# Output matrices that begin with the rows already at hand, and a head norm taken by group

## The reference, cut to what matters

```
# even mixer (layer 0)
o = o_fwd + o_bwd                                  # delta rule, 8 heads of 128
o = o * rsqrt(mean(o*o, -1) + eps) * out_gain
y_dn = o * silu(gate)                              # 1024 columns
y_sc = b_gate * centred_dwconv(c_gate * u_in)      # 1024 columns, no delta result in it
return concatenate([y_dn, y_sc]) @ w_out           # [256, 2048] @ [2048, 2048]

# odd mixer (layer 1)
y_c = sum(wts * outs)                              # attention, 512 columns
y = ys[0] + ys[1]                                  # RWKV both ways, 8 heads of 64
yn = (y - mean) * rsqrt(var + eps) * ln_w + ln_b   # mean, var over a head
y_d = (yn + bonus) * gate                          # 512 columns
return concatenate([y_c, y_d]) @ w_out             # [256, 1024] @ [1024, 2048]
```

## Time and profile before

| | us |
|---|---|
| three runs | 3073.96, 3075.31, 3089.07 |
| median | 3075.31 |
| profiled execution, its own time | 3086.94 |
| span of the profiled execution | 3084.9 |
| PE busy | 2899.5 (94%) |
| DVE busy | 1569.9 (51%) |
| ACT busy | 1270.4 (41%) |
| POOL busy | 186.1 (6%) |
| mean granted PE clock | 0.955 |

### The profile page before, as it was taken

How to read it: one execution, slowest core, us unless ns; L and a number is a source line. 1 busy time by engine, 2 the same in 40 slices (tenths; PEclk the granted TensorE clock), 3 DMA queues, 4 the chain that set the end, 5 groups by cost and what they waited for, 6 DMA issues and landing times.

```text
span 3084.9 us, 45243 instructions
## 1 busy us (share of the span) xinstructions
PE 2899.5 (94%) x18708; PEld 2662.6 (86%) x18708; DVE 1569.9 (51%) x1923; ACT 1270.4 (41%) x1564; POOL 186.1 (6%) x169
## 2 busy tenths in 40 slices
PE   7999989899999999999899986888799999999999
PEld 7999988788898989899798984888688989898897
DVE  4555455555554454444545556443655444544444
ACT  4543322364543534444444443112455434444343
POOL 0000055100000000000000001432000000000000
PEclk9999989899999999999999997877899999999999
DMA  6455300254455455555445550001344545545444
GB/s 250 165 191 183 132 1 1 109 178 150 151 191 192 179 195 187 191 184 186 150 174 187 193 177 17 1 1 55 109 164 141 187 178 179 193 175 191 178 179 149
DMA packets 67915, 462.26 MB, mean 150 GB/s; under 512 B 7007, under 2 KB 10079, under 8 KB 12940
## 3 DMA queue, kind: packets, MB, share of 16 engines
q1 hardware_dynamic: 63680, 449.95, 40.7%
q10 hardware_dynamic: 3500, 5.21, 0.5%
q0 software_dynamic: 544, 4.19, 0.4%
HBM read 457.21 MB, written 5.27 MB: 150 GB/s over the span
## 4 chain that ended last, share of the span: by engine, by line
PE 91%; DVE 5%; ACT 2%; issue 1%; POOL 0%; DMA 0%; ACTq 0%; DVEq 0%; POOLq 0%
PE bank L401 13%; PE bank L402 13%; PE bank L403 13%; PE bank L376 12%; PE bank L378 12%; PE bank L377 12%; PE bank L1020 3%; PE bank L1004 3%; PE bank L1988 1%; PE bank L1211 1%; PE bank L502 1%; ACT split_hi L320 1%; DVE hT_lo L515 0%; DVE split_lo L327 0%; PE bank L1709 0%
## 5 line engine op out<-in xcount | busy, mean ns | idle before, releaser
L327 DVE TENSOR_TENSOR split_lo<-raw,split_hi 128x1024 fp32r<-128x1024 f32 x840 | 1026.6, 1225 | 1113.2 <-ACT split_hi L320 1112.3
L320 ACT ACTIVATE split_hi<-raw 128x1024 fp32r<-128x1024 f32 x840 | 888.2, 1059 | 1312.9 <-PE bank L403 696.8
L401 PE MATMUL bank<-hT_hi,split_hi 128*128 128x256 f32 x3376 | 963.2, 285 | 23.0 <-issue 11.4
L402 PE MATMUL bank<-hT_lo,split_hi 128*128 128x256 f32 x3376 | 961.3, 285 | 0.0
L403 PE MATMUL bank<-hT_hi,split_lo 128*128 128x256 f32 x3376 | 961.1, 285 | 0.0
L401 PEld LDWEIGHTS bank<-hT_hi,split_hi 128*128 128x128 f32 x3376 | 654.4, 194 | 26.8 <-issue 17.9
L402 PEld LDWEIGHTS bank<-hT_lo,split_hi 128*128 128x128 f32 x3376 | 654.5, 194 | 0.2
L403 PEld LDWEIGHTS bank<-hT_hi,split_lo 128*128 128x128 f32 x3376 | 654.3, 194 | 0.0
L376 PE MATMUL bank<-split_hi,u_hi 128*128 128x512 f32 x1152 | 449.4, 390 | 0.0
L377 PE MATMUL bank<-split_lo,u_hi 128*128 128x512 f32 x1152 | 448.3, 389 | 0.0
L378 PE MATMUL bank<-split_hi,u_lo 128*128 128x512 f32 x1152 | 448.3, 389 | 0.0
(11 more groups left out here) (391 smaller groups left out, 2290.3 us busy)
## 6 DMA issues: line engine op xcount, KB each, us to landing
raw<-in_stream SPq DMA_DIRECT2D x420, 1024.0 KB, 4.8
work<-in_mem POOLq DMA_DIRECT2D x2, 2048.0 KB, 8.0
bias_rows<-bias_line SPq DMA_DIRECT2D x1, 3072.0 KB, 14.0
hwork<-bias_rows ACTq DMA_DIRECT2D x2, 1536.0 KB, 9.5
x<-in_x SPq DMA_DIRECT2D x1, 2048.0 KB, 8.9
out<-x SPq DMA_DIRECT2D x4, 512.0 KB, 5.0
const<-in_masks SPq DMA_DIRECT2D x1, 1665.5 KB, 12.4
work<-in_wide ACTq DMA_DIRECT2D x1, 1280.0 KB, 6.2
```

What stands on the lines that cost most here:

```text
L320: nc.scalar.activation(split_hi[:, u % SPLIT], raw[:, b % RAW, (u % 2) * UNIT:(u % 2 + 1) * UNIT], ACT.Copy).then_inc(s_hi, 1)
L327: nc.vector.tensor_tensor(split_lo[:, u % SPLIT], raw[:, b % RAW, (u % 2) * UNIT:(u % 2 + 1) * UNIT], f32(split_hi[:, u % SPLIT]), SUB).th ...
L401: nc.tensor.matmul(out, lhsT=w_hi[:, cols], rhs=hT_hi[:, k, :], start=k == 0, stop=False)
L402: nc.tensor.matmul(out, lhsT=w_hi[:, cols], rhs=hT_lo[:, k, :], start=False, stop=False)
```

## The change

Even mixer: the rows of `ev_out` are stored with the short convolution's 1024 rows first, and PE reads k tile (k + 8) mod 16. `yscT` is written to `hT` in four pieces right after ACT's last copy of the delta tail, and DVE takes the low parts before the last group's output. PE starts chunk 0 on these tiles and turns the heads after units 2 and 3 of that chunk (8 transposes each). Units 4 and 5 are split before the heads' tiles are written. The last group's output goes to bank 2 in place of bank 0, since chunk 0 writes banks 0 and 1.

Odd mixer: the norm's sum, mean, square and variance are taken for each group right behind the copy of its output. The root and the rest of the norm are taken for groups 0 to 2 together, in the last group, and for group 3 at the end. The weights of the norm, the bonus and the gate are folded into two tensors by POOL in groups 0 and 1: `y_add = (bonus * v + ln_b) * gate` and `gout = gate * ln_w`. PE turns the first two tiles before chunk 0 and the other two after unit 1. Its waits are by tile.

```diff
+            def turn_heads(u):
+                if u not in (2, 3):
+                    return
+                pe.wait_ge(s_y, u - 1)
...
+            pe_out_cross(pe, 0, "ev_out", KD, lambda k, t: hT_tile((k + 8) % KD, t),
+                         lambda k: pe.wait_ge(s_yT, k // 2 + 1), turn_heads)
...
+        OUT_BANK = (0, 0, 0, 2)
...
             act_delta_tail(act, DN_GROUPS - 1, range(3))
+            act.wait_ge(s_qtg, 2 * DN_GROUPS)
+            for b in range(4):
+                nc.scalar.activation(hT_hi[:, 8 + 2 * b:10 + 2 * b, :], yscT[:, 2 * b:2 * b + 2, :], ACT.Copy).then_inc(s_ysp, 1)
             act.wait_ge(s_oms, 1)
             nc.scalar.activation(o_sd, o_ms, ACT.Sqrt).then_inc(s_osd, 1)
+            hi_upto(act, starts["ev_out"][1] + AHEAD + 2)
             act.wait_ge(s_o, 4)
-            nc.scalar.activation(hT_hi[:, 8:16, :], yscT, ACT.Copy).then_inc(s_ysp, 1)
...
+            turn_heads(0)
+            pe_out_cross(pe, 1, "od_out", 8, hT_tile, lambda k: pe.wait_ge(s_yT, 9 + k // 2),
+                         lambda u: turn_heads(1) if u == 1 else None)
...
+                    if f + 1 == RW_F and level == 5:
+                        act.wait_ge(s_oms, RW_F)
+                        nc.scalar.activation(norm_of(gsd, 0, 3), norm_of(gms, 0, 3), ACT.Sqrt).then_inc(s_osd, 1)
...
             dve_rwkv_state(dve, RW_F - 1)
+            dve_rwkv_norm(dve, 0, 3, 2)
+            for b in range(2):
+                dve.wait_ge(s_ysp, b + 9)
+                nc.vector.tensor_tensor(hT_lo[:, 2 * b:2 * b + 2, :], ycT[:, 2 * b:2 * b + 2, :],
+                                        f32(hT_hi[:, 2 * b:2 * b + 2, :]), SUB).then_inc(s_yT, 1)
             dve_rwkv_out(dve, RW_F - 1)
...
+            dve_step(nc.vector.reduce_sum(norm_of(gsum, f, 1), y, AX_X))
+            dve_step(nc.vector.tensor_scalar(norm_of(gmean, f, 1), norm_of(gsum, f, 1), 1.0 / RW_N, None, MULT))
+            dve_step(nc.vector.tensor_tensor(y, y, wide_of(gmean, f, 1), SUB))
+            dve_step(nc.vector.tensor_tensor(y_heads(y_sq, 0, 1), y, y, MULT))
+            dve_step(nc.vector.reduce_sum(norm_of(gvar, f, 1), y_heads(y_sq, 0, 1), AX_X))
+            nc.vector.tensor_scalar(norm_of(gms, f, 1), norm_of(gvar, f, 1), 1.0 / RW_N, GN_EPS, MULT, ADD).then_inc(s_oms, 1)
...
+        def dve_rwkv_norm(dve, f, n, root):
+            dve.wait_ge(s_osd, root)
+            dve.wait_ge(s_gnw, 1)
+            y, own = y_heads(Ytok, f, n), slice(f * P, (f + n) * P)
+            dve_step(nc.vector.reciprocal(norm_of(grs, f, n), norm_of(gsd, f, n)))
+            dve_step(nc.vector.tensor_tensor(y, y, wide_of(grs, f, n), MULT))
+            dve_step(nc.vector.tensor_tensor(Ytok[:, :, own], Ytok[:, :, own], gout[:, :, own], MULT))
+            nc.vector.tensor_tensor(Ytok[:, :, own], Ytok[:, :, own], y_add[:, :, own], ADD).then_inc(s_y, 1)
...
+                    if f < 2 and level in (2, 3):
+                        pool_norm_weights(pool, 2 * f + level - 2)
```

More of the change, by code:

```diff
@@ L275, in build @@
             sem(n) for n in ("s_rc", "s_rF", "s_rRA", "s_rbk", "s_rM", "s_rMAT", "s_rbt", "s_rBK", "s_rz1", "s_rz1s"))
-        s_gms, s_gsd, s_ry, s_ryt = (sem(n) for n in ("s_gms", "s_gsd", "s_ry", "s_ryt"))
+        s_gnw = sem("s_gnw")
         block = ctx.enter_context(nc.Block())
@@ L1176, in pe_even @@
                 pe_delta_tail(pe, DN_GROUPS - 1, step)
[L1177 to L1184, removed]
+            def turn_heads(u):
+                if u not in (2, 3):
+                    return
+                pe.wait_ge(s_y, u - 1)
+                for b in range(2 * u - 4, 2 * u - 2):
+                    for i in range(2):
+                        for t in range(NT):
+                            m = nc.tensor.transpose(aux[b][:, (2 * i + t) * P:(2 * i + t + 1) * P],
+                                                    y_tok[:, t, 2 * b + i, :], ident)
+                    m.then_inc(s_yt, 1)
+            pe_out_cross(pe, 0, "ev_out", KD, lambda k, t: hT_tile((k + 8) % KD, t),
+                         lambda k: pe.wait_ge(s_yT, k // 2 + 1), turn_heads)
         DN_GROUPS = 4
+        OUT_BANK = (0, 0, 0, 2)
         PRE_SLOT = (5, 9)
@@ L1251, in pe_delta_tail @@
                     for i in range(2):
-                        out = bank[0][:, (2 * t + i) * P:(2 * t + i + 1) * P]
+                        out = bank[OUT_BANK[hp]][:, (2 * t + i) * P:(2 * t + i + 1) * P]
                         qkt = QKT[hp % 2]
@@ L1475, in dve_even @@
             dve_delta_R(dve, DN_GROUPS - 1)
+            for b in range(4):
+                dve.wait_ge(s_ysp, b + 1)
+                nc.vector.tensor_tensor(hT_lo[:, 8 + 2 * b:10 + 2 * b, :], yscT[:, 2 * b:2 * b + 2, :],
+                                        f32(hT_hi[:, 8 + 2 * b:10 + 2 * b, :]), SUB).then_inc(s_yT, 1)
             dve_delta_out(dve, DN_GROUPS - 1)
@@ L1487, in dve_even @@
                 nc.vector.tensor_tensor(y_tok[:, :, own, :], y_tok[:, :, own, :], g4, MULT).then_inc(s_y, 1)
-            dve.wait_ge(s_ysp, 1)
-            nc.vector.tensor_tensor(hT_lo[:, 8:16, :], yscT, f32(hT_hi[:, 8:16, :]), SUB).then_inc(s_yT, 1)
+            lo_upto(dve, starts["ev_out"][1] + AHEAD + 2)
             for b in range(4):
-                dve.wait_ge(s_ysp, b + 2)
+                dve.wait_ge(s_ysp, b + 5)
                 nc.vector.tensor_tensor(hT_lo[:, 2 * b:2 * b + 2, :], aux[b][:, :].rearrange("p (h s) -> p h s", s=S),
@@ L1880, in build @@
         SD = W(17408, 2, P)
-        Ytok = mem_v[0]
+        Ytok, y_sq = mem_v[0], mem_v[1]
+        y_add = mem_kT[1].rearrange("p h s -> p (h s)").rearrange("p (t n) -> p t n", t=NT)
         mid_w, side_w = st[:, 336:351], st[:, 352:367]
@@ L1945, in pe_rwkv, with turn_heads @@
                 pe_rwkv_tail(pe, RW_F - 1, step)
-            pe.wait_ge(s_ry, 1)
-            for b in range(2):
+            def turn_heads(b):
+                pe.wait_ge(s_y, b + 3)
                 for i in range(2):
@@ L2041, in pe_rwkv_tail @@
                     d2 = 1 if t == 0 else 0
-                    nc.tensor.matmul(bank[0][:, t * P:(t + 1) * P], lhsT=ra[:, d2, t, 1], rhs=SD[:, d2], start=True, stop=False)
+                    nc.tensor.matmul(bank[OUT_BANK[f]][:, t * P:(t + 1) * P], lhsT=ra[:, d2, t, 1], rhs=SD[:, d2], start=True, stop=False)
                     for d in range(2):
@@ L2247, in pool_rwkv_pre, with pool_norm_weights @@
                 nc.gpsimd.tensor_tensor(ktl[f % 2][:, d], f_cols(kdT[:, d], f), Fx[:, d, :, 2, :], MULT).then_inc(s_rbk, 1)
+        def pool_norm_weights(pool, step):
+            row = lambda j: ln_wb[:, j].unsqueeze(1).broadcast_to([P, NT, RW_W])
+            if step == 0:
+                pool.wait_ge(s_bon, 1)
+                pool.wait_ge(s_rv, 2)
+                pool.wait_ge(s_rgs, 2)
+                pool.wait_ge(s_wide, 32)
+                pool_step(nc.gpsimd.tensor_tensor(y_add.rearrange("p t (h e) -> p (t h) e", e=RW_N),
+                                                  rv.rearrange("p t (h e) -> p (t h) e", e=RW_N),
+                                                  lanes(bon.rearrange("p t h -> p (t h)"), RW_N), MULT))
+            elif step == 1:
+                pool_step(nc.gpsimd.tensor_tensor(y_add, y_add, row(1), ADD))
+            elif step == 2:
+                pool_step(nc.gpsimd.tensor_tensor(y_add, y_add, gout, MULT))
+            else:
+                nc.gpsimd.tensor_tensor(gout, gout, row(0), MULT).then_inc(s_gnw, 1)
         def pool_odd(pool):
```

65 lines of the change are left out of this document (26 added, 39 removed).

## The result

| | before | after |
|---|---|---|
| median, lowest to highest, runs | 3082.1 us, 3073.96 to 3089.07, 4 | 3040.05 us, 3032.5 to 3048.71, 4 |
| profiled execution: own time, span, PE's mean clock | 3086.94, 3084.9, 0.955 | 3032.61, 3030.8, 0.964 |

A forecast was written before the change was run, and what follows sets the result against it. PE's chain of waits was taken as the bound (91% of the span). Even mixer 10.5 + odd mixer 17.0 - recurrence 0.2 = 27.3 us; 27 off the 3075.31 us median gave 3048, range 3040 to 3064.

The forecast's parts named there:

- Start: Even mixer: PE starts chunk 0 right behind the delta tail, at 575.3 in place of 586.41, 11.1 us earlier.
- Transposes inside: Even mixer: the 16 head transposes stay on PE, now inside chunk 0, and cost 1.9 us at the fast level.
- Slow start: Even mixer: chunk 0's first matmuls ran at the low clock level; without a pause this 1.25 us is saved.
- covers: Even mixer: both head halves hidden by at least 2.1 us; heads' low parts from DVE by about 0.7 us.
- slow matmuls after: Odd mixer: low level may last into chunk 0 after the change, costing 0 to 3.3 us, taken as 2.0.
- Rival 1: Clock takes part back: low level costs even chunk 0 7.0 us, odd 3.3; gain 19 us, 3056; chance 0.14.
- -0.2: RWKV's recurrence: DVE's added norm work costs 0.2 us in all; POOL's four new operations taken as 0.
- two places: The stretches ahead of the even and odd output matrices, where PE waits; gains of 10.5 and 17.0 us.
- Rival 5: Whole kernel: runs span 15 us; if the next median falls with the long ones, 3062; chance 0.07.
- rival 3: Recurrence: POOL's four operations hold DVE at full length, 11.6 us lost, gain 16, 3059; chance 0.02.
- cover of 2.7 us: RWKV's first group: level 4's masks from POOL, at about 1946.2, come 2.7 us before PE wants them.
- rival 4: Recurrence: PE's inversions wait for masks behind POOL's new operations, from about 4.3 us each; slower, 3091; chance 0.03.

The follow-up runs named there:

- even_only: The kernel before with only the change's even mixer, odd mixer as before: 3079.91 us, ratio 0.9986.
- odd_only: The kernel before with only the change's odd mixer, even mixer as before: 3059.44 us, ratio 0.9922.
- before_pad1: The kernel before with one long-met wait added on PE ahead of the second feed-forward part's loop: 3074.64 us, one run.
- after_pool4: The changed kernel with the first of POOL's four new operations (bonus product, 128x1024) done four times over: 3049.53 us, one run.
- after_hold: The changed kernel with PE waiting ahead of each output matrix until all heads are normed and gated: 3047.65 us, ratio 0.9902.

## Why the prediction was right, and where it was not

**Even mixer, right in each term.** Start: 575.2 to 586.41 became 576.4 to 576.38, so 11.2 earlier (said: 11.1). Transposes inside: from the matmul ahead of them to the second behind them 1.34 us each time, where two steps take 0.45, so 1.8 in all (said: 1.9). Slow start: 1.25, by the rows of before. Sum 10.65. Measured 10.6, the same 10.6 in `even_only`, and 11.0 the other way round when the pause was put back. Its covers held.

**Odd mixer, right.** Start 16.7 earlier (said: 16.8); four transposes, measured in the same way, 0.45 (0.7); slow matmuls of before 2.9 (2.9); slow matmuls after, 2138.85 to 2143.6, 4.75 x 0.465 = 2.2 (the 2.0 taken between 0 and 3.3). Sum 16.95, measured 16.9 and 16.4 in `odd_only`. Rival 1 had the mechanism for this mixer and no part in the even one: without a pause the level did not fall.

**Recurrence, right in the code's share and silent on the clock's.** The -0.2 was for DVE's and POOL's added work, and in 234.6 us against the 234.6 us of `before_pad1` it is 0.0. The difference of the profiled pair, 12.3, is low time: 26.2 us less of it, at 0.46. The step that failed is that the two places' "waits don't hang on what made it longer, so I take the same 27 us off the median". It was true of the two stages, but the median of three runs, 3075.31, is itself the shorter kind, and after's four runs are two of each (3032.5 twice, 3047.5 and 3048.7), so its median is a mean of the two kinds. With the fourth run of before (3088.89) the same is true of 3082.1, so the 42 us between these two medians is a fair measure. Rival 5 saw runs 15 us apart and had no cause for them.

**FFN1, not seen.** The sum, 27.3, lacks a term of 16.8. The trace of before showed the three `issue` waits in the loop, but they stand in no stage that the diff touches. Like for like the change is worth 3075 - 3032.5 = 42.5 us: 27.5 as costed, 16.8 by the loop's position, less 1 to 2 of small differences. That the median stayed in the range, by 0.05 us, is luck: the missing term made it 16.8 us better, and half of the runs at the longer recurrence made it 7.5 worse. Four runs of the shorter kind would have given 3032.5, below the range. The two places were costed rightly; the total was not.

**POOL, right by less than was claimed.** The operations took 1.90 to 2.36 us, inside 2.9, and L1057 kept its 0.42 beside them, so rival 3's price was not paid. One reading behind that rival is loose: the 0.68 us called "alone" were not, since POOL's masks began at 1929.68, 0.16 us behind DVE's operation. In that row DVE had begun first, in the row of 1.74 us POOL had. But the cover of 2.7 us was read at level 4 in a trace whose PE ran slower. In the trace after level 4 has 1.0 us, and `after_pool4` made level 3 wait. The point of rival 4, 4.3 us an operation, was too high: by the trace after it is about (1.90 + 2.35 + 1.0) / 2 = 2.6.

## What to carry to other kernels

- Order the rows of a matrix so that it begins with those that exist, and read the gain as start to start plus what the low level costs the first matmuls. Both sums came out within 0.1 us in the profiled pair and within 0.6 in the runs with one mixer. The second term is no constant: 1.25 us before, 2.5 in `after_hold`, by how much of the low stretch falls on matmuls.
- Look through the whole span for `issue` waits at a loop's turn, also where the diff does nothing: the odd mixer's edit removed them here without touching the loop. Three empty waits were worth 16.7 us in this stage, so tell such a gain from the edit's own by a control that only shifts the code.
- When runs fall into two groups, compare them group by group and cut the traces by stage with the low time of each. Idle times of PE amid small products (2 to 13 us here) are worth filling, best if the filler ends with the wait; take the filler's length from a trace, since 24 products took 5.6 us and not 3.

## What the runs showed of the hardware

- A loop of PE with 4 turns had 3 idle times of 3.6 to 4.0 us, one between each two turns, and at each of them one 16 KB instruction packet more, 163 in the run for 160; they went with three more instructions ahead of it, not with one.
- Each came with 3.4 to 6.8 us at the low level, so 11.4 us of idle time cost 16.8.
- The recurrence has two lengths, 234.6 (before_pad1, after, after_hold) and 250.3 to 250.9 us (the seven profiled runs of the other experiments without filling), with 88 and 117 to 125 us at the low level. The profiled run of before, 246.9, went from one to the other. The groups are then 58.0 and 61.4 us long, with 23.9 and 30.7 us low in each. What chooses is open.
- Filling the idle time took the low part of the recurrence from 87.8 to 36.6 us, but only 13.6 us off its length (234.6 to 221.0), where 51 us of slow matmuls would be worth 24 at 0.46 each. How the rest divides between idle time and the filler's own time was not measured.
